# Moving the first index scores and ten top-k picks between the chunks of the query, key and value projections

## The reference, cut to what matters

```
q, k, v, qi, ki, wi = split_cols(pa, ATT_SPLITS)
q = rope(rms_norm(q, q_norm), pos);  k = rope(rms_norm(k, k_norm), pos)
qi = rope(qi, pos);  ki = rope(ki, pos)
logits = jnp.einsum('bqhd,bsd->bqhs', qib, ki)          # 8 index heads of 64
score = jnp.einsum('bqhs,bqh->bqs', jax.nn.relu(logits), wib)
_, idx = lax.top_k(score, n_sel)                        # 128 keys of each query
p = softmax(q k^T * scale over the picked keys);  o = p v
```

## Time and profile before

| | before |
|---|---|
| median of three runs | 3707.87 us |
| the profiled execution | 3705.42 us, span 3703.6 us |
| PE (TensorE) busy | 3608.6 us, 97% |
| DVE (VectorE) busy | 1938.7 us, 52% |
| ACT (ScalarE) busy | 1497.7 us, 40% |
| POOL (GpSimd) busy | 1653.4 us, 45% |
| mean granted TensorE clock | 0.992 of full speed |

### The profile page before, as it was taken

One profiled execution on the slowest core, in us unless ns is written; L12 is line 12 of the kernel. 1 busy time (PEld: TensorE's weight loads), 2 busy tenths in 40 slices (PEclk: granted clock), 3 DMA queues, 4 the chain that ended last, 5 costly groups with the idle time before them and its releaser, 6 DMA issues.

```text
span 3703.6 us, 55820 instructions
## 1 busy us (share of the span) xinstructions
PE 3608.6 (97%) x23122; PEld 2998.2 (81%) x23122; DVE 1938.7 (52%) x3397; ACT 1497.7 (40%) x2673; POOL 1653.4 (45%) x936
## 2 busy tenths in 40 slices
PE   9999999999899999999999999999999999999999
PEld 8877888888788878888767888888888876788887
DVE  2356554344645544552676635543553396655552
ACT  3444333434433343333455343334333455534332
POOL 3114566421266635664322335663666322235664
PEclk9999999999999999999999999999999999999999
DMA  4103332311243234323210034323332320012332
GB/s 129 41 29 97 114 100 66 95 52 35 67 135 100 69 101 128 101 69 89 75 46 2 3 118 123 103 64 120 104 103 75 88 57 24 3 42 90 99 103 97
DMA packets 393405, 291.95 MB, mean 79 GB/s; under 512 B 17056, under 2 KB 355904, under 8 KB 393152
## 3 DMA queue, kind: packets, MB, share of 16 engines
q1 hardware_dynamic: 387728, 284.49, 25.2%
q10 hardware_dynamic: 5136, 2.70, 0.3%
q0 software_dynamic: 288, 1.18, 0.1%
HBM read 286.24 MB, written 2.10 MB: 78 GB/s over the span
## 4 chain that ended last, share of the span: by engine, by line
PE 83%; DVE 10%; ACT 4%; POOL 2%; issue 1%; ACTq 0%; DMA 0%; DVEq 0%; SPq 0%; POOLq 0%
PE ps L823 13%; PE ps L824 13%; PE ps L825 13%; PE ps L1052 4%; PE ps L1053 4%; PE ps L1054 4%; PE ps L955 3%; PE ps L952 3%; PE ps L954 3%; PE ps L1080 2%; PE ps L1612 2%; PE ps L1100 2%; PE ps L1089 1%; PE ps L1162 1%; PE ps L1227 1%
## 5 line engine op out<-in xcount | busy, mean ns | idle before, releaser
L3461 POOL TENSOR_TENSOR wl<-wraw,wh 128x1024 fp32r<-128x1024 f32 (+1 forms) x424 | 1025.7, 2424 | 1555.5 <-ACT wh L2776 1552.1
L823 PE MATMUL ps<-x_T,wh 128*128 128x512 f32 (+1 forms) x2224 | 850.3, 382 | 0.0
L824 PE MATMUL ps<-x_T,wh 128*128 128x512 f32 (+1 forms) x2224 | 849.0, 382 | 0.0
L825 PE MATMUL ps<-x_T,wl 128*128 128x512 f32 (+1 forms) x2224 | 849.0, 382 | 0.0
L2776 ACT ACTIVATE wh<-wraw 128x1024 fp32r<-128x1024 f32 (+1 forms) x424 | 445.8, 1052 | 763.1 <-PE ps L825 489.9
L823 PEld LDWEIGHTS ps<-x_T,wh 128*128 128x128 f32 x2224 | 418.7, 188 | 81.4 <-POOL wl L3461 0.7
L824 PEld LDWEIGHTS ps<-x_T,wh 128*128 128x128 f32 x2224 | 418.6, 188 | 80.5 <-issue 0.5
L825 PEld LDWEIGHTS ps<-x_T,wl 128*128 128x128 f32 x2224 | 418.6, 188 | 80.4
L2060 DVE TENSOR_TENSOR scr<-scr,ps 128x512 f32<-128x512 f32 x132 | 90.6, 686 | 465.8 <-ACT scr L2931 465.8
L1052 PE MATMUL ps<-wh,h_T 128*128 128x512 f32 x672 | 262.4, 390 | 0.2
L1053 PE MATMUL ps<-wl,h_T 128*128 128x512 f32 x672 | 261.5, 389 | 0.0
(11 more groups left out here) (822 smaller groups left out, 6876.7 us busy)
## 6 DMA issues: line engine op xcount, KB each, us to landing
wraw<-in_ffn_w_gate_dram SPq DMA_DIRECT2D x88, 512.0 KB, 3.9
wraw<-in_ffn_w_up_dram SPq DMA_DIRECT2D x88, 512.0 KB, 3.9
wraw<-in_w_in_dram SPq DMA_DIRECT2D x82, 512.0 KB, 3.7
wraw<-in_w_gate_dram SPq DMA_DIRECT2D x44, 512.0 KB, 3.9
wraw<-in_w_up_dram SPq DMA_DIRECT2D x44, 512.0 KB, 3.9
mix<-in_ffn_w_down_dram SPq DMA_DIRECT2D x20, 1024.0 KB, 6.8
arena<-in_ffn_w_down_dram SPq DMA_DIRECT2D x12, 1024.0 KB, 6.4
wraw<-in_ffn_w_down_dram SPq DMA_DIRECT2D x24, 512.0 KB, 3.7
```

The source lines that it names most:

```text
L823: mm(b[:, t0:t1], wh[:, k, :], xTh[:, k, t0:t1], k == 0, False)
L824: mm(b[:, t0:t1], wh[:, k, :], xTl[:, k, t0:t1], False, False)
L825: ins = mm(b[:, t0:t1], wl[:, k, :], xTh[:, k, t0:t1], False, k == 7)
L3461: tt(wl, raw_of(w), wh.bitcast(F32), ALU.subtract).then_inc(*g.sig("w", "lo", w))
```

## The change

TensorE, ScalarE and VectorE enter a new function, `early_rounds`, between the 336-column projection and the loop; GpSimd passes through it doing nothing. TensorE projects one chunk (weight tile) of the queries, makes the index transposes (`index_heads`), four index scores, a chunk, four scores, a chunk, two scores, the last chunk of the queries, and the two chunks of keys and values. VectorE ropes, accumulates the eight scores of tile 3 and makes two, four and four of its picks. ScalarE stages weights in `chunks`, copies the queries out after their last chunk, and squares them behind `early_rounds`. The four PSUM banks of a projection are held while other work stands between its chunks. In the head rounds `top` takes a step as well. The loop goes on with the same lanes, so it begins with eighteen index steps and fourteen picks done. `WAITS`, weight order and loads are untouched.

```diff
--- before.py
+++ after.py
@@ -356,6 +356,18 @@
 COLS2 = (6, 0, 1) + tuple(range(7, 13)) + (2, 3, 4, 5)
 
 
+def early_rounds(proj, heads, index, top):
+
+    next(proj)
+    heads()
+    for scores, picks in ((4, 0), (4, 0), (2, 2), (0, 4), (0, 4)):
+        for _ in range(scores):
+            next(index)
+        for _ in range(picks):
+            next(top)
+        next(proj)
+
+
 def project_lane(piece, work):
 
 
@@ -782,6 +795,32 @@
             def use():
                 wat[0] += 1
                 return wat[0] - 1
+
+            def chunks_T(*widths):
+
+                for n in widths:
+                    ws, kk = [], WCH // n
+                    for c in range(8 // kk):
+                        ws.append(use())
+                        if c == 0:
+                            last = ws[0] + 8 // kk - 1
+                            bks = [bank(("Tm", last, j), ("ev", last, j), hold=True) for j in range(NT)]
+                            for _, free in bks:
+                                pe.wait_ge(*free)
+                        wh, wl = hl_of(ws[c])
+                        pe.wait_ge(*at("w", "lo", ws[c]))
+                        for q in range(kk):
+                            k = c * kk + q
+                            for j in range(NT):
+                                o = bks[j][0][:, 0:n]
+                                mm(o, xh(k, j), wh[:, q, :], k == 0, False)
+                                mm(o, xh(k, j), wl[:, q, :], False, False)
+                                ins = mm(o, xl(k, j), wh[:, q, :], False, k == 7)
+                        ins.then_inc(*pe.sig("w", "used", ws[c]))
+                        if k == 7:
+                            for j in range(NT):
+                                held.discard(book.bank[("Tm", last, j)])
+                        yield
 
             def to_T(name, src, ready, tiles=range(NT)):
                 for j in tiles:
@@ -1753,18 +1792,16 @@
                        behind=partial(to_T, *rms, (2, 3)))
                 pass_by(4)
                 proj_T(8, 336, xh, xl)
-                proj_T(8, 512, xh, xl)
-                index_heads(l)
-                proj_T(8, 256, xh, xl)
                 masks, summed, stock = set(), set(), Stock(l)
+                index = index_lane(0, summed, lambda i, h: index_sum(l, i, h))
+                top = top_lane(summed, masks, nothing, nothing, nothing)
+                early_rounds(chunks_T(512, 256), lambda: index_heads(l), index, top)
 
                 def over():
                     pe.mark("dsa over", l)
                     stock.open()
 
-                mixer_rounds(heads(l), lambda h, i: unit3(l, ("dsa", h, i)),
-                             index_lane(0, summed, lambda i, h: index_sum(l, i, h)),
-                             top_lane(summed, masks, nothing, nothing, nothing),
+                mixer_rounds(heads(l), lambda h, i: unit3(l, ("dsa", h, i)), index, top,
                              project_lane(piece_F, last_F), gates(l),
                              [rec_tile(l, j, stock) for j in range(4)], masks, over)
                 outputs(l)
@@ -2689,7 +2726,10 @@
                 ts(omu, colat[("rwkv_mu_2", l)], -1.0, 1.0, ALU.mult, ALU.add).then_inc(*v.sig("omu", l))
                 use(tiles_of(8, 512))
                 use(tiles_of(8, 336))
-                index_heads(l)
+                masks, summed, stock = set(), set(), Stock(l)
+                index = index_lane(2, summed, partial(index_sum, l))
+                top = top_lane(summed, masks, partial(top_first, l), partial(top_step, l), partial(top_last, l))
+                early_rounds(rests(6), partial(index_heads, l), index, top)
                 use(tiles_of(8, 512))
                 use(tiles_of(8, 256))
                 v.wait_ge(*at("ev", where["w_in_2", l, ((1280, 72), (3016, 264))], 3))
@@ -2697,7 +2737,6 @@
                 step(tt(ga, gz[:, :, 260:264], bc(rows["dt"].unsqueeze(1), [P, 4, 4]), ALU.add))
                 step(ts(gt, ga, -1.0, None, ALU.mult))
                 tt(gt, gt, ga, ALU.max).then_inc(*v.sig("rec", "gabs", l))
-                masks, summed, stock = set(), set(), Stock(l)
 
                 def over():
                     v.mark("dsa over", l)
@@ -2708,9 +2747,7 @@
                     v.memset(Ms[0], 0.0).then_inc(*v.sig("rec", "M0", l))
                     v.wait_ge(*v.own())
 
-                mixer_rounds(heads(l), lambda h, i: unit3(l, ("dsa", h, i)),
-                             index_lane(2, summed, partial(index_sum, l)),
-                             top_lane(summed, masks, partial(top_first, l), partial(top_step, l), partial(top_last, l)),
+                mixer_rounds(heads(l), lambda h, i: unit3(l, ("dsa", h, i)), index, top,
                              project_lane(nothing, partial(project, l)), rests(16),
                              [rec_tile(l, j, stock) for j in range(4)], masks, over)
                 barrier("o", l)
@@ -3372,6 +3409,19 @@
                     small_dma(vup[0:32, :], A["rwkv_v_up_2"][0]).then_inc(*s.dma("lora", l, 3))
                 small_dma(lora[64:128, :], A["rwkv_g_up_2"][l]).then_inc(*s.dma("lora", l))
 
+            def chunks(l):
+                for _ in range(3):
+                    use()
+                    yield
+                w = use()
+                for j in range(NT):
+                    s.wait_ge(*at("w", "used", w))
+                    copy(qtm2[:, j, :], psum_of("Tm", w, j)[:, :]).then_inc(*s.sig("ev", w, j))
+                yield
+                for _ in range(2):
+                    use()
+                    yield
+
             def block2(l):
                 ffn(2 + 2 * l, partial(lifts, l))
                 rms_norm(l, 1, lambda i, half: ("ffn", "x", 2 + 2 * l, 1, half, i))
@@ -3383,12 +3433,12 @@
                     copy(kitm[:, j, :], b[:, 0:64])
                     copy(wiv[:, j, :], b[:, 64:72], scale=8 ** -0.5 * 64 ** -0.5)
                     copy(gz[:, j, :], b[:, 72:336]).then_inc(*s.sig("ev", w, j))
+                masks, summed, stock = set(), set(), Stock(l)
+                index = index_lane(1, summed, partial(index_sum, l))
+                top = top_lane(summed, masks, nothing, nothing, nothing)
+                early_rounds(chunks(l), partial(index_heads, l), index, top)
                 s.wait_ge(*at("dsa", "ropek", l))
-                w = use(tiles_of(8, 512))
-                for j in range(NT):
-                    s.wait_ge(*at("w", "used", w))
-                    copy(qtm2[:, j, :], psum_of("Tm", w, j)[:, :]).then_inc(*s.sig("ev", w, j))
-                index_heads(l)
+                w = where["w_in_2", l, 0]
                 for j in range(NT):
                     s.wait_ge(*at("ev", w, j))
                     act(scr[j][:, :], qtm2[:, j, :], ACT.Square).then_inc(*s.sig("dsa", "sq", l, j))
@@ -3398,22 +3448,19 @@
                 act(sml(53)[:, 0:4], rows["al"], ACT.Exp).then_inc(*s.sig("rec", "al", l))
                 step(act(gt, gt, ACT.Exp, scale=-1.0))
                 act(gt, gt, ACT.Ln, bias=1.0).then_inc(*s.sig("rec", "gln", l))
-                w = use(tiles_of(8, 256))
+                w = where["w_in_2", l, 512]
                 for j in range(NT):
                     s.wait_ge(*at("w", "used", w))
                     b = psum_of("Tm", w, j)
                     act(scr[4][:, j * P:(j + 1) * P], b[:, 0:128], ACT.Square).then_inc(*s.sig("dsa", "sqk", l))
                     copy(ktm2[:, j, :], b[:, 0:128])
                     copy(vv[:, j, :], b[:, 128:256]).then_inc(*s.sig("ev", w, j))
-                masks, summed, stock = set(), set(), Stock(l)
 
                 def over():
                     s.mark("dsa over", l)
                     stock.open()
 
-                mixer_rounds(heads(l), lambda h, i: unit3(l, ("dsa", h, i)),
-                             index_lane(1, summed, partial(index_sum, l)),
-                             top_lane(summed, masks, nothing, nothing, nothing),
+                mixer_rounds(heads(l), lambda h, i: unit3(l, ("dsa", h, i)), index, top,
                              project_lane(nothing, partial(project, l)), gates(l),
                              [rec_tile(l, j, stock) for j in range(4)], masks, over)
                 barrier("o", l)
@@ -3629,6 +3676,9 @@
                 stage(wat[0] + AHEAD)
                 use(13)
                 masks, summed, stock = set(), set(), Stock(l)
+                index = index_lane(0, summed, nothing)
+                top = top_lane(summed, masks, nothing, nothing, nothing)
+                early_rounds(rests(6), nothing, index, top)
 
                 def over():
                     g.mark("dsa over", l)
@@ -3639,8 +3689,7 @@
                     if k == COLS2[-1]:
                         stage(wat[0] + AHEAD + 1)
 
-                mixer_rounds(rests(4), lambda h, i: rests(4), index_lane(0, summed, nothing),
-                             top_lane(summed, masks, nothing, nothing, nothing),
```

(1 more changed line is left out.)

## The result

The changed kernel takes **3748.69 us** (median of 4 runs, 3746.43 to 3754.41), the kernel before in the same session 3704.14 (4 runs). The ratio is 1.0126, 95% interval 1.0113 to 1.0138: slower, by 44.6 us, where 9 were forecast. The profiled execution took 3747.98 us.

The account below looks back on a forecast made before the run. The prediction took TensorE and VectorE both to be near the bound, on a chain of waits between engines. Its terms, 14.0 + 1.5 - 11.0 = +4.5 us a layer, +9.0 in all, gave 3714 us, range 3692 to 3735.

Parts of the forecast that it names:

- Terms 1 to 3: Ahead of round 0: queries 8.9 us later, squares 4.6 us later still, head rounds +0.5; round 0 14.0 us late.
- Term 2: Ahead of round 0: ScalarE squares the queries only after passing both key chunks, so the squares come 4.6 us later still.
- term 3: Head rounds: more picks and accumulations, less 3.5 us of VectorE's waits for GpSimd's weight conversions; sum +0.5 us.
- Term 4: Rounds 0 to 36: rounds 0 to 15 gain 5.5 us, the rest takes 59 us for 52; +1.5 us a layer.
- Units were moved into rounds where TensorE is full: Rounds 16 to 36: tile 3's units start in round 16 instead of 18; the stretch takes 59 us for 52.
- + 4 for table loads: Rounds from 16 on: 4 us for table loads within the 47 us reckoned for tile 3's units.
- Term 5: From round 37 until tile 1 of the recurrence is made: picks and units end earlier, 76 us for 87, -11 us.
- `over` within 3 us of its time before: Sign that the forecast is right: VectorE's memsets after the last units come within some 3 us of their time before.
- TensorE's wait ahead of round 0: Slower rival: a longer rest there drops the clock and warm-ups delay without helping; +6.9 us a layer, 3728 us, chance 0.12.
- VectorE as the bound wherever it picked: Faster rival: rounds 0 to 15 go at VectorE's 32.6 us, later rounds gain too; -7.6 a layer, 3690 us, chance 0.23.

Follow-up runs that it names:

- e8_transposes: The changed kernel with no scores or picks between the query chunks, only the index transposes early: 3703.99 us, ratio 1.0003.
- e14_tr_squares: e8_transposes with ScalarE's squares directly behind the copies of the queries, ahead of the key chunks: 3702.32 us, ratio 1.0001.
- e1_moved: The changed kernel with only the warm-up matmuls in the attention units of tiles 3 and 2 re-placed: 3719.37 us, ratio 1.0047.
- e7_no_picks: e5_squares with no picks before the head rounds, the ten early scores still there: 3753.17 us, ratio 1.0127.
- e10_seven_two: e7_no_picks with 8 warm-ups more, ahead of the transposes of unit (7,2): 3725.89 us, ratio 1.0061.
- e5_squares: e1_moved with ScalarE's squares directly behind the copies of the queries, ahead of both key chunks: 3729.44 us (3710.54 to 3740.72).

## Why the prediction was wrong

**Terms 1 to 3** stood: from chunk 0 to round 0 it is 86.7 / 88.2 us instead of 72.3 / 72.4, 14.4 and 15.7 more, forecast 14.0; the queries were copied out 9.1 us later and the first reduction started 13.8 us later, as said. Inside, parts cancelled, which is luck. The transposes cost 2.2, not 3.8 (e8_transposes), the scores with their waits 6.8, not 5.1. Term 2 was priced alone at 4.6 but is worth nothing by itself (e14_tr_squares): later ropes meet fewer conversions. The 3.5 us that term 3 gave back for these is 5.8: in the changed kernel's first layer one hit of 2.1 us and one of 0.8 are left where four cost 8.7.

**Term 4**: rounds 0 to 15 gained 4.1 us where 5.5 were forecast. Behind them the term failed in one step, and it is the main one: "Units were moved into rounds where TensorE is full" was counted (+7, and e1_moved has +6.1), the warm-ups only as matmuls in rounds 0 to 15. That the units leave the table loads of the gates behind was written down as "+ 4 for table loads", as if they kept their cover. That cost 9.1 / 6.0 us (67.6 and 64.4 for 58.4): in the first layer 2.3, 1.4 and 0.7 us of warm-ups of (5,3), (0,2) and (1,2) that cover nothing, and the half clock behind the waits of 1.7, 1.1 and 2.4 us.

**Term 5** had the (3,2) warm-ups in the right round but at full clock (3 us, measured 5.9 at the 1.2 GHz level), and missed the wait of 2.33 us at (5,2), behind another pair of table loads. With the warm-ups re-placed the stretch gains 8.0 / 6.6 us of the 11 forecast; without, it gains 2.6 in the first layer and loses 1.3 in the second. In e1_moved it is 47.3 / 50.1 us from round 36 to `over`, where 47 were forecast, and 31.6 / 32.1 from there to tile 1, where 29 were: the mechanism stands, and most of what was over-counted in the first layer is in the second part. The sign that the prediction gave for itself failed by a wide margin: `over` within 3 us of its time before, and it came 18.3 us later (2017.9 for 1999.5).

**The rivals.** The third, "TensorE's wait ahead of round 0", had the right mechanism with 0.12 of the chance and 6.9 us a layer. The clock did fall ahead of round 0 in both layers, as it said, but e1_moved keeps these falls (0.50 from 1851 to 1860, around round 0) and loses none of its 29 us by them; the waits that count are in rounds 16 to 44, most of them for exponentials behind table loads. The size was wrong too (14.2 and 15.4 us a layer, the changed kernel's sums less those of e1_moved). The Trainium skill, "TensorE: Matmul & The Clock Gate", section "HAM oscillation", tells of an array that falls back in waits for DMA of some 3 to 5 us; the trace agrees in kind, but here it fell behind waits of 1.0 to 2.4 us for ScalarE. VectorE as the bound wherever it picks is out for rounds 0 to 15: its busy time there is 31.8 us, as reckoned (32.6), but the rounds take 37.4, not 32.6.

In sum: 44.6 us are 29 by warm-ups and clock (e1_moved), and 15 to 17 by early scores and picks that the head of the phase can't hide (e8_transposes, without them, is level with the kernel before), against the 9 forecast. The range ended at 3735 because the forecast followed only one of the seven entries of `WAITS` behind round 16 to its new round, and no rival counted the waits that the others left uncovered.

## What to carry to other kernels

Fillers tuned by hand are keyed to something; before moving work, write down for each one which wait it covers and whether filler and wait move together. If they are keyed to units and the waits to rounds, re-place them in the same edit, or the trial measures the fillers. And price a term on a chain of engines with what its shift does to their contention, since here (e8_transposes) the squares came 3.7 us later behind the queries and VectorE's way from them to the keys was 4.4 us shorter, by the two conversions that it no longer met.

## What the runs showed of the hardware

In e7_no_picks a single TensorE wait of 1.03 us was followed by some 37 us at a granted 0.50 (1981 to 2018, and 3169 to 3206 in the second layer), under a mix of narrow matmuls during which the profile shows TensorE idle for 1.28 us alone; 8 warm-ups of 128x384 ahead of the wait kept 1.00 from 1985 to 2000 through the same work (e10_seven_two). Waits of like length don't always do it: 1.19 us ahead of unit (1,3) were followed by 1.00 in the kernel before, and in e8_transposes, ahead of the same unit, by this:

```profile
1903.00:1906.00 3.00, 3.00 (x9) 0.50 0.00 0
```

What decides between the two, no run here shows. So two kernels with the same wait can differ by microseconds of half clock, and a single execution of an order with such waits says little. Whether the 30 us of spread of e5_squares come from such a wait was not shown.
